# The first weight tiles of a stage run on the input without its reciprocal root, among the steps of the normalisation

## What is computed

```python
def rms_norm(x, g, eps=NORM_EPS):
    xf = x.astype(jnp.float32)
    y = xf * lax.rsqrt(jnp.mean(xf * xf, axis=-1, keepdims=True) + eps)
    return (y * g.astype(jnp.float32)).astype(x.dtype)
...
x = x + mixer(rms_norm(x, norm_mix_g[l]) , ...)
x = x + ffn(rms_norm(x, norm_ffn_g[l]), ...)
```

## Time and profile before

| | us |
|---|---|
| median of 3 runs | 2570.45 (2568.37 to 2571.87) |
| the profiled execution, its time | 2566.45 |
| the profiled execution, span from first to last instruction | 2564.7 |
| TensorE busy in it | 2380.3 |
| VectorE busy in it | 1648.9 |
| ScalarE busy in it | 987.6 |
| mean granted clock of TensorE | 0.956 |

### The profile page before, as it was taken

The page is one execution under the profiler, slowest core; times in us unless marked ns, Lnnn a source line. Parts: engine busy times, 40 slices in busy tenths (PEclk is TensorE's granted clock), DMA queues, the critical chain, the costliest instruction groups (busy, mean ns, idle before and its releaser), DMA issues. The chain is left out here.

```text
span 2564.7 us, 47617 instructions
## 1 busy us (share of the span) xinstructions
PE 2380.3 (93%) x20452; PEld 2311.8 (90%) x20452; DVE 1648.9 (64%) x2750; ACT 987.6 (39%) x1441; POOL 187.9 (7%) x300
## 2 busy tenths in 40 slices
PE   7889989799899999999778999998999998988999
PEld 7889988799899999899558999998999998967999
DVE  6768887679777777734684677776333335376554
ACT  6446544465533222322472332223222223146443
POOL 0000000180000000011000900000000000100000
PEclk9889998899989999999898999999999998989999
DMA  6236753267535555412001455552222322112464
GB/s 250 83 132 210 234 197 116 91 196 252 183 107 198 188 192 197 173 58 78 14 1 66 161 188 193 198 192 80 92 98 100 99 96 94 67 50 67 157 196 157
DMA packets 104305, 352.77 MB, mean 138 GB/s; under 512 B 18976, under 2 KB 19232, under 8 KB 103840
## 3 DMA queue, kind: packets, MB, share of 16 engines
q1 hardware_dynamic: 95904, 348.94, 39.5%
q0 software_dynamic: 8192, 0.80, 0.3%
HBM read 348.63 MB, written 1.05 MB: 136 GB/s over the span
## 5 line engine op out<-in xcount | busy, mean ns | idle before, releaser
L1371 ACT ACTIVATE W_hi<-W_raw 128x1024 fp32r<-128x1024 f32 x510 | 539.7, 1061 | 1119.1 <-PE slot L888 1033.4
L1717 DVE TENSOR_TENSOR W_lo<-W_raw,W_hi 128x1024 fp32r<-128x1024 f32 x510 | 622.0, 1223 | 515.8 <-ACT W_hi L1371 506.9
L886 PE MATMUL slot<-H_hiA,W_lo 128*128 128x256 f32 x2864 | 815.1, 285 | 18.9 <-DVE H_loA L1827 6.6
L887 PE MATMUL slot<-H_loA,W_hi 128*128 128x256 f32 x2864 | 806.6, 282 | 0.0
L888 PE MATMUL slot<-H_hiA,W_hi 128*128 128x256 f32 x2864 | 805.9, 281 | 0.0
L886 PEld LDWEIGHTS slot<-H_hiA,W_lo 128*128 128x128 f32 x2864 | 553.0, 193 | 28.1 <-issue 21.6
L887 PEld LDWEIGHTS slot<-H_loA,W_hi 128*128 128x128 f32 x2864 | 553.8, 193 | 0.1
L888 PEld LDWEIGHTS slot<-H_hiA,W_hi 128*128 128x128 f32 x2864 | 552.9, 193 | 0.0
L1729 DVE SCALAR_TENSOR_TENSOR PROD<-A_raw,SC 128x1024 bf16<-128x1024 f32 x288 | 341.2, 1222 | 151.9 <-DMA A_raw<-adastream 151.4
L886 PE MATMUL slot<-H_hiB,W_lo 128*128 128x256 f32 x1280 | 356.9, 279 | 4.4 <-DVE VB L2199 4.4
L887 PE MATMUL slot<-H_loB,W_hi 128*128 128x256 f32 x1280 | 356.0, 278 | 0.0
(11 more groups left out here) (269 smaller groups left out, 3048.6 us busy)
## 6 DMA issues: line engine op xcount, KB each, us to landing
W_raw<-wstream SPq DMA_DIRECT2D x510, 512.0 KB, 3.3
A_raw<-adastream SPq DMA_DIRECT2D x144, 512.0 KB, 4.4
BT<-par POOLq DMA_DIRECT2D x256, 3.0 KB, 2.7
XA<-xT SPq DMA_DIRECT2D x2, 512.0 KB, 4.5
SC<-cond SPq DMA_DIRECT2D x1, 1024.0 KB, 14.4
XB<-ctxT SPq DMA_DIRECT2D x1, 1024.0 KB, 16.4
CON<-const SPq DMA_DIRECT2D x1, 960.5 KB, 9.5
PAR<-par SPq DMA_DIRECT2D x1, 680.0 KB, 10.7
```

The source lines that it names most:

```text
L886: pe.matmul(out, wl, xh, start=start, stop=False, skip_group_check=True)
L887: pe.matmul(out, wh, xl, start=False, stop=False, skip_group_check=True)
L1371: act.activation(W_hi[:, g % HIGH, :], W_raw[:, g % RAW, :], ACT.Copy).then_inc(S.w_hi, 1)
L1717: dve.tensor_tensor(W_lo[:, g % RAW, :], W_raw[:, g % RAW, :], W_hi[:, g % HIGH, :].bitcast(F32), ALU.subtract).then_inc(S.w_lo, 1)
```

## The change

At the four norms of the first block (mixer and ffn, two layers) the first macro of the stage behind the norm is computed from H0 = X x gain, without the root, and the four blocks in PSUM are multiplied by the root once it is known. H0_hi and H0_lo lie in the space of the second stream's H, which the first block doesn't use.

- `weave` mixes the four visits of the norm with the first four of the next stage: n0, t0, t1, n1, t2, n2, t3, n3. The tiles of the first macro come in the order 0, 2, 1, 3, so that t0 and t1 use kt = 0 to 3, t2 and t3 use kt = 4 to 7. On TensorE t0 and t1 are ahead of the sums, t2 is between sums and spread, t3 behind the spread.
- ScalarE makes eight H0_hi in the first piece, ahead of or among the squares, and copies the spread root to ROOT in SBUF. VectorE makes eight H0_lo, and `rooted` multiplies the macro by ROOT (1024 columns of PSUM).
- At the program's start the splits of the first three tiles stand behind the whole first piece of the norm.
- The macro of mix1 lies in the glue slots (PSUM slots 2 and 3), and glue numbers count to 13 for a layer.
- `place_ada`: mix1 has its pairs at the third- and fourth-last visit; before, at the fourth-last and in layer 1 also at the first two.
- Nothing is changed in POOL's functions.

```diff
+def weave(visits):
+    out, i = [], 0
+    while i < len(visits):
+        if visits[i].stage.kind == "norm" and visits[i].stage.early is not None:
+            n, u = visits[i:i + 4], visits[i + 4:i + 8]
+            out += [n[0], u[0], u[1], n[1], u[2], n[2], u[3], n[3]]
+            i += 8
+        else:
+            out.append(visits[i])
+            i += 1
+    return out
...
         if st.kind == "mix1":
-            v.ada = int(left == 4 or (st.l > 0 and v.i < 2))
+            v.ada = int(left in (3, 4))
...
+            def early(s, st, b, q):
+                wl, wh = weights()
+                for t in range(2):
+                    for k in range(4):
+                        kt = 4 * (q % 2) + k
+                        if t == 0 and q < 2:
+                            pe.wait_ge(S.h0_ready, KT * st.early + kt + 1)
+                        c = slice(256 * k + P * t, 256 * k + P * t + P)
+                        mm = three(b[:, 2 * (q // 2) + t, :], wl[:, c], wh[:, c], H0_lo[:, kt, :], H0_hi[:, kt, :],
+                                   kt == 0 and t == 0, kt == 7)
+                mm.then_inc(s.sem.done, 1)
...
+            def early_squares(s, st):
+                if st.old is None:
+                    act.wait_ge(S.x_in, 32)
+                    act.wait_ge(S.head_in, 32)
+                else:
+                    act.wait_ge(s.sem.evac, st.old.tok)
+                early_half(s, st, 0, 4)
+                act.activation(s.SQ[0][:, :, :], s.X[:, 0:4, :], ACT.Square).then_inc(s.sem.squared, 1)
+                if st.old is not None:
+                    act.wait_ge(s.sem.upd, st.upd + 1)
+                early_half(s, st, 4, 6)
+                if st.old is not None:
+                    act.wait_ge(s.sem.evac, st.old.tok + 1)
+                early_half(s, st, 6, 8)
+                act.activation(s.SQ[1][:, 0:2, :], s.X[:, 4:6, :], ACT.Square).then_inc(s.sem.squared, 1)
+                act.activation(s.SQ[1][:, 2:4, :], s.X[:, 6:8, :], ACT.Square).then_inc(s.sem.squared, 1)
...
+                if st.early is not None:
+                    act.wait_ge(s.sem.spread, st.rs + 1)
+                    act.activation(ROOT[:, :], ps(st, norm_token(st))[:, 1, 0:SEQ], ACT.Copy).then_inc(S.root_out, 1)
...
-                if 1 <= n <= AHEAD:
-                    split(n - 1)
+                if n == 1:
+                    for g in range(AHEAD):
+                        split(g)
...
+            def rooted(s, st, b):
+                dve.wait_ge(s.sem.done, st.v + 4)
+                dve.wait_ge(S.root_out, st.early + 1)
+                dve.tensor_tensor(b[:, :, :], b[:, :, :], bcast_mid(ROOT[:, :], 4), ALU.mult).then_inc(S.rooted, 1)
...
+                if st.early is not None:
+                    early_low(s, st, 0, 4)
                 finish_update(s, st)
+                if st.early is not None:
+                    early_low(s, st, 4, 8)
                 add_squares(s, st)
```

More of the change, by code:

```diff
@@ L148, in __init__ @@
         self.late, self.proj = late, proj
+        self.early = None
+        if blk == 1 and kind == "norm" or kind == "mix1":
+            self.early = 2 * l + which
+        if blk == 1 and kind == "ffn":
+            self.early = 2 * l + 1
         self.tok = count["tok"]
@@ L203, in ffn @@
         for a, b in GROUPS:
-            steps += [up_unit(l, blk, which, m, q) for m in range(a, b) for q in range(4)]
+            steps += [up_unit(l, blk, which, m, q) for m in range(a, b)
+                      for q in ((0, 2, 1, 3) if blk == 1 and m == 0 else range(4))]
             steps += [down_unit(l, blk, which, half, j) for half in range(2) for j in range(a, b)]
@@ L588, in build_kernel @@
         B.SG = at("SGB", AB + 24 * K, [P, 2 * SEQ])
+        H0_hi, H0_lo = B.H_hi, B.H_lo
+        ROOT = at("ROOT", AB, [P, SEQ])
         U = at("U", AA + 24 * K, [P, 4, SEQ])
@@ L670, in wait, with up_token, norm_token @@
             eng.wait_ge(sem, value)
+        def up_token(st, i, m):
+            first = st.tok + (i and GROUPS[0][1] - GROUPS[0][0] + 2)
+            return first + m - (st.early is not None and i == 0 and m == 0)
+        def norm_token(st):
+            return st.tok + (st.early is not None and st.which == 1)
         def groups1(st):
             causal = con("causal", 512)
-            toks = (6, 7, 8, 9)
+            toks = (7, 8, 9, 10)
             out = []
@@ L959, in norm @@
                 yield
-                yield
+                if st.early is None:
+                    yield
             def final(s, st):
@@ L973, in ffn @@
                     for m in range(a, b):
+                        if st.early is not None and m == 0:
+                            pe.wait_ge(s.sem.evac, st.tok - 2)
+                            pe.wait_ge(S.glue, GLUE * (st.l + 1))
+                            for q in (0, 2, 1, 3):
+                                early(s, st, blocks(st, st.tok - 1), q)
+                                yield
+                            tok += 1
+                            continue
                         open_token(s, st, tok)
@@ L1835, in norm @@
                     dve.wait_ge(S.gain_ready, 3 * st.l + st.which + 1)
-                dve.wait_ge(s.sem.spread, st.rs + 1)
+                root = p[:, 1, 0:SEQ]
+                if st.early is None:
+                    dve.wait_ge(s.sem.spread, st.rs + 1)
+                else:
+                    dve.wait_ge(S.root_out, st.early + 1)
+                    root = ROOT[:, :]
+                    if st.which == 0:
+                        release(S.root_out, st.early + 1, s.sem.evac, tok)
                 scale(0)
@@ L2361, in _ @@
             for n, v in enumerate(ORDER):
-                if 2 <= n < 2 + AHEAD:
-                    split(n - 2)
+                if n == 1:
+                    for g in range(AHEAD):
+                        split(g)
                 if n == FIRST_STEPS:
```

114 lines of the change are left out of this document (68 added, 46 removed).

## The result

Over four runs the changed kernel takes a median of 2627.4 us (2620.68 to 2632.33), against 2569.41 over four runs of the kernel before. The ratio is 1.0209, with a 95% interval of 1.0169 to 1.0249: slower, as forecast. 1.0209 times the 2570.45 from which the prediction started is 2624, the top of its range; the median itself is 3.4 us above it. The two medians lie 58.0 us apart.

The account below looks back on a forecast made before the run. TensorE (93% busy) was taken as the bound, its longest first-block waits belonging to norms, with VectorE's chain counting in the mixer's middle. Terms +2.9 -3.9 -5.6 +51.9 = +45.3 on 2570.45 gave 2615 us; 8 in 10: 2600 to 2624.

Parts of the forecast that it names:

- N3: Norm before the second up projection: root's guess waits on POOL behind the bias table's memset and 128 issues; loss 52.
- The issues' price: POOL's 128 bias-table DMA issues at N3: 0.477 us each, 61.1 in all, even with VectorE idle.
- Rival D: At N3 the DMA issues go faster beside an idle VectorE; at half their price +15, 2585 us; chance 0.04.
- N1: Norm before the first up projection: early tiles fill the gap, t8 starts at +28.6 instead of +32.5; gain 3.9.
- N2: Norm before the second mixer: t6 ends at 375.5 instead of 381.1; gain 5.6, or 3 if VectorE can't catch up.
- N0: Norm at the program's start: the condition's silu on ScalarE delays t4's split, root and low halves; loss 2.9.
- without the silu it would be a gain of about 1: Start norm: with the condition's silu out of the way on ScalarE, the loss of 2.9 becomes a gain of about 1.
- rival B: Root behind table; low-half waits in t4, t5 lower the clock, N1 and N2 lose up to 3; +54 to +65; 0.09.
- The likeliest case: Root behind the table (+52), other three norms together between gain 18 and loss 2; +34 to +54; chance 0.78.

Follow-up runs that it names:

- half the issues: Changed kernel with 64 of the 128 DMA issues of POOL's first bias table left out; 2582.34 us profiled, ratio 1.0087 to the kernel before.
- the table behind the root: Changed kernel with POOL starting the bias table at the fifth visit of the ffn behind N3, not the first; 2570.81 us profiled, ratio 0.9985 to the kernel before.
- the run of 2598.57: Changed kernel with bias table and silu issued later, and N0's squares, sums and root ahead of its first tile; longest of 12, median 2571.06, ratio 0.9972.

## Why the prediction was right, and where it was short

**N3, POOL's queue: right, and shown.** Forecast +52; t8 came at 585.40 against 532.46, less the 1.05 us by which the mixer ended later: +51.9. Undoing the order gives it all back, putting it alone into the kernel before makes it, and taking half of the issues away takes 30.3 us off it.

**The issues' price: right.** 61.07 us for 128 with VectorE at 0.00 in 510 to 520, 61.10 where it was busy; 22 issues in 10 us in both. Rival D is dead. The rule of the Trainium skill (DMA: Bandwidth & Descriptors, SWDGE vs HWDGE vs iDMA) is that VectorE in its two-port mode locks POOL out of the SBUF state that it writes descriptors to, so that issues would go faster beside an idle VectorE. No run shows that here. What VectorE ran beside the 61.10 us were `tensor_tensor` and `scalar_tensor_tensor` in float32, 25.7 us of them the splits with two inputs in SBUF; in which port mode they ran the trace doesn't tell.

**N1 and N2: right.** From the last matmul in front to t8 are 28.35 us at N1 against 32.81, a gain of 4.5 (forecast 3.9); at N2 the shift falls from +6.5 to +1.1 at the gate logits, 5.4 (forecast 5.6). So close a hit at N2 is partly luck: the same stretch, from the last matmul in front to the gate logits, takes 30.63, 32.04 and 30.95 us in the three profiles of before and 25.21 to 26.92 in the four with the change as made. The product of 1024 columns, priced at 1.25 by bounds, takes 1.23.

**N0: direction right, term mis-sized, and its step wrong.** Forecast +2.9; +6.4 and +5.9 at the gate logits (+4.9 with half the issues, whose N0 is the same). By its steps: the silu ended at 23.72 and its split at 24.67, as counted (23.8, 24.9), but the variance would have waited for the sums behind t0 and t1 anyhow (behind the split it still waited 0.38 us for them), and "without the silu it would be a gain of about 1" failed: without it the loss is still 5.7. What was missed: a table load of 1.28 us on ScalarE, done at 0.74 before, now stands behind the landing of PAR (t0 at 16.80, not 15.5); ROOT ends at 29.84, not 28.8, since the spread stands behind t2; a split and the sinks' products stand among the low halves (last one at 38.37, not 36.9); and the wait in t4 costs the clock, 28 matmuls at 0.21. That last is rival B's mechanism. It came at N2 as well, where TensorE waits 1.7 us in t4: in the changed kernel's second profile and with the table behind the root the granted clock is 0.83 in 370 to 380, in the first profile 1.00. From the gate logits to the mixer's root another -1.5 to +1.4 us come in (the kernel before takes 72.5 to 74.0 us there). Four profiles with this N0 have the root at 117.38, 118.41, 121.64 and 121.79; between 80 and 110 the granted clock is 0.83 in the first two and 0.72 in the last two, and 0.11 of 30 us is 3.3 us, most of the difference. Why the clock stayed low for longer there is open.

**The range.** The likeliest case was the one that came. Its sum of +45.3 was 5.9 short of the +51.2 at the first block's end, of which N0 gave 3.6 (at the gate logits) to 5.0 (at the mixer's root); the range's top was 3.4 under the median. By the number alone the medians' +58.0 would be rival B's (+54 to +65), but B's N1 and N2 lose, and here they gain. The rest, up to the profile's +62.5 at the end, came between 1480 and 1820, where the changed kernel's first profile ran at the slower pace: the same matmul is 50.9 us late at 1480 and 62.3 at 1820.

## What to carry to other kernels

An engine that is 7% busy can be the bound: a write that nobody waits for, issued one small piece at a time, holds everything behind it in the same queue (here a guess of 0.7 us, whose input was ready at 509.95, started at 565.93). When steps are interleaved anew, read the order on each queue, the small ones too, and put long issue runs behind the last operation that a busy engine waits for. Early work pays only where the engine had been idle and where its helpers' queues (splits, low halves, a table load) don't wait for something later; at the start of a program that is a late transfer.

## What the hardware showed beyond that

- In these runs TensorE has a second pace at a granted clock of 1.00: 172 instead of 179 matmuls of 256 columns in 20 us, 4% slower (one every 0.118 us instead of 0.113), in spells of 40 to over 600 us, at other places in each run of the same kernel. In these profiles it accounts for up to an estimated 44 us (56 of 78 full stretches in the run of 2598.57, at 0.78 us). In the rows shown neither DMA share (0.58 and 0.55 in 220 to 240) nor the other engines' load tells the paces apart; no run tests a cause, and it is open.
- 128 DMA issues on POOL of 3 KB each take 0.48 us apiece on its queue (61.07 to 61.32 us), busy neighbours or idle ones.
